# Prompt attention: coefficients transposed whole, masked by VectorE and spread by one 128x512 product

## The reference, cut to what matters

```python
p_c = masked_softmax(jnp.einsum('bqghd,bngd->bghqn', qg, kc) * scale, mask_c)   # 32 compressed keys
o_c = jnp.einsum('bghqn,bngd->bqghd', p_c.astype(vc.dtype), vc)
...
p_s = masked_softmax(jnp.einsum('bqghd,bgqkd->bghqk', qg, kg) * scale, mask_s)  # selected blocks
o_s = jnp.einsum('bghqk,bgqkd->bqghd', p_s.astype(vg.dtype), vg)
...
p_w = masked_softmax(jnp.einsum('bqghd,blgd->bghql', qg, kw) * scale, mask_w)   # last 512 keys
o_w = jnp.einsum('bghql,blgd->bqghd', p_w.astype(vw.dtype), vw)
g = gates.reshape(b, qb, 3, NSA_KV_HEADS, NSA_HG, 1)
o = g[:, :, 0] * o_c + g[:, :, 1] * o_s + g[:, :, 2] * o_w
```

## Time and profile before

| | us |
|---|---|
| runs before | 2155.36, 2158.88, 2159.72 |
| median | 2158.88 |
| the profiled execution | 2153.33 |
| its span, first to last instruction | 2151.6 |
| prompt attention, from its first product to its last scaling | 430.7 to 731.7 |

### The profile page before, as it was taken

One profiled execution on the slowest core, in us unless ns is written; L12 is line 12 of the kernel. 1 busy time (PEld: TensorE's weight loads), 2 busy tenths in 40 slices (PEclk: granted clock), 3 DMA queues, 4 the chain that ended last, 5 costly groups with the idle time before them and its releaser, 6 DMA issues. The chain is left out here.

```text
span 2151.6 us, 25397 instructions
## 1 busy us (share of the span) xinstructions
PE 1876.8 (87%) x10730; PEld 1266.2 (59%) x10730; DVE 693.7 (32%) x1200; ACT 524.9 (24%) x1001; POOL 286.9 (13%) x209
## 2 busy tenths in 40 slices
PE   4499949699889799979997959997999999978795
PEld 4245537366666566656665547774668855534694
DVE  1321110256555234434443231114301124432524
ACT  1400110155444321123343200015311112320004
POOL 1011000011100000024453420000000000010410
PEclk9699979889999899999998979998999999988898
DMA  9101083100000101200001454333110010004312
GB/s 345 72 0 68 1 204 84 42 1 2 1 1 1 44 20 40 98 4 1 1 1 30 124 175 149 110 121 143 40 39 20 20 40 1 1 30 137 120 40 81
DMA packets 116901, 131.83 MB, mean 61 GB/s; under 512 B 15926, under 2 KB 93912, under 8 KB 116148
## 3 DMA queue, kind: packets, MB, share of 16 engines
q1 hardware_dynamic: 95572, 104.94, 15.3%
q10 hardware_dynamic: 20864, 25.17, 3.4%
q0 software_dynamic: 352, 0.10, 0.1%
HBM read 104.83 MB, written 27.43 MB: 61 GB/s over the span
## 5 line engine op out<-in xcount | busy, mean ns | idle before, releaser
L154 PE MATMUL banks<-h_T,w_xbc 128*128 128x352 f32 x576 | 170.9, 460 | 0.0
L154 PE MATMUL banks<-w_attn,h_T 128*128 128x512 f32 (+5 forms) x432 | 160.1, 533 | 0.0
L154 PEld LDWEIGHTS banks<-h_T,w_xbc 128*128 128x128 f32 x576 | 109.5, 190 | 60.9 <-issue 0.6
L154 PE MATMUL banks<-w_r,h_T 128*128 128x512 f32 (+1 forms) x288 | 129.0, 602 | 0.0
L154 PE MATMUL banks<-w_z_b,h_T 128*128 128x512 f32 (+1 forms) x288 | 126.2, 597 | 0.0
L154 PE MATMUL banks<-w_qkv,h_T 128*128 128x256 f32 (+1 forms) x576 | 125.6, 380 | 0.5 <-ACT h_T L2045 0.5
L154 PEld LDWEIGHTS banks<-w_attn,h_T 128*128 128x128 f32 (+1 forms) x432 | 78.5, 183 | 80.3 <-issue 63.5
L154 PEld LDWEIGHTS banks<-w_qkv,h_T 128*128 128x128 f32 (+1 forms) x576 | 103.9, 181 | 22.4 <-issue 2.6
L154 PE MATMUL banks<-h_T,w_qkv 128*128 128x352 f32 x384 | 114.5, 460 | 0.0
L1143 DVE TENSOR_REDUCE neg_max_att<-banks 128x1 f32<-128x640 f32 (+7 forms) x128 | 89.2, 702 | 73.7 <-PE banks L154 73.4
L154 PE MATMUL banks<-conv_T,out_even_w 128*128 128x352 f32 x288 | 92.0, 470 | 14.2 <-DMA out_even_w<-in_w_out_even_dram 12.9
(11 more groups left out here) (427 smaller groups left out, 2977.4 us busy)
## 6 DMA issues: line engine op xcount, KB each, us to landing
out_even_w_mod<-in_w_mod_dram ACTq DMA_DIRECT2D x8, 2048.0 KB, 9.5
h_T<-x_T_save SPq DMA_DIRECT2D x2, 4224.0 KB, 16.8
w_qkv<-in_w_in_odd_dram SPq DMA_DIRECT2D x8, 1024.0 KB, 5.4
w_xbc<-in_w_in_even_dram SPq DMA_DIRECT2D x6, 1024.0 KB, 5.3
x_T_save<-x_T SPq DMA_DIRECT2D x1, 4224.0 KB, 23.6
x_T_save<-h_T SPq DMA_DIRECT2D x1, 4224.0 KB, 19.2
xin<-in_x_prompt_dram SPq DMA_DIRECT2D x2, 2048.0 KB, 16.0
h_T<-in_w_mod_dram SPq DMA_DIRECT2D x2, 2048.0 KB
```

The costliest lines, as they stand in the source:

```text
L154: return nc.tensor.matmul(out, lhsT, rhs, start=start, stop=stop, skip_group_check=True)
```

## The change

`turn_coef` becomes one ordinary transpose of a 128x128 tile: `coef_att` has 128 columns for a block and branch, of which DVE fills the first 8, and POOL sets all to zero once. DVE then multiplies the transposed tile (in PSUM) by a mask into `coef_wide`, 128x512: column block hh keeps the two heads hh and hh+4 (`widen`). A new `spread_coef` is one product with a 0/1 matrix (`half`), contraction over 128 partitions, 512 columns. Mask and matrix lie in a new tile `spread`, 128x132, which SP loads at the start of the stage; PE and DVE wait for it there.

A closing now has two places: the transpose (`turns`) in the unit where the eight products were, the product (`fins`) one unit later. Both stand ahead of `values(n - 1)`. A closing takes two numbers in the counter of groups: the transpose's goes to DVE, the product's to ACT.

```diff
+F_COLS["half"], F_COLS["pick"] = (F_WIDTH + SH, F_WIDTH + SH + P), (F_WIDTH + SH + P, F_WIDTH + SH + P + HG)
...
+    put(f, F_COLS, "half", (p < H)[:, None] & (p[:, None] // HG == p[None, :] // HD))
+    put(f, F_COLS, "pick", (p < H)[:, None] & (p[:, None] % HG == np.arange(HG)[None, :]))
...
-        fins[at["att", i, 0, 0]].append((i, 0))
-        fins[at["att", i, 1, 0]].append((i, 1))
-        fins[at["cmp", i + 1, 0, 0] if i + 1 < NTP else len(units) - 1].append((i, 2))
+        for kind, n in enumerate((at["att", i, 0, 0], at["att", i, 1, 0], at["cmp", i + 1, 0, 0] if i + 1 < NTP else len(units) - 1)):
+            turns[n].append((i, kind))
+            fins[min(n + 1, len(units) - 1)].append((i, kind))
...
+        for eng, table, some in ((0, turning, turns[n]), (1, closing, fins[n])):
+            for f in some:
+                table[f] = len(engine_of)
+                engine_of.append(eng)
...
+        den, coef = sb("den_att", [P, 2, 3, H]), sb("coef_att", [P, 2, 3, P])
+        spread, wide = sb("spread", [P, P + HG]), sb("coef_wide", [P, 2, HG, P])
...
+                sp.dma_start(spread[:, :], e.k_f32[:, F_COLS["half"][0]:F_COLS["pick"][1]]).then_inc(spread_in, 16)
...
                 def turn_coef(i, kind):
 
-                    g = closing[i, kind]
+                    g = turning[i, kind]
                     pe.wait_ge(coef_ready, 3 * i + kind + 1)
                     wait_copied(pe, g - 2)
-                    for hh in range(HG):
-                        for half in range(G):
-                            h = half * HG + hh
-                            c = coef[:, i % 2, kind, h:h + 1].broadcast_to([P, HD])
-                            last = mm(nc, e.ps[half * HD:(half + 1) * HD, 4 + g % 2, hh * P:(hh + 1) * P], c, e.ident, True, True)
-                    last.then_inc(t_done, 1)
+                    nc.tensor.transpose(e.ps[:, 4 + g % 2, 0:P], coef[:, i % 2, kind, :], e.ident).then_inc(t_done, 1)
+
+                def spread_coef(i, kind):
+
+                    g = closing[i, kind]
+                    wait_copied(pe, turning[i, kind])
+                    wait_copied(pe, g - 2)
+                    mm(nc, e.ps[:, 4 + g % 2, :], spread[:, 0:P], wide[:, (3 * i + kind) % 2, :, :].rearrange("p h t -> p (h t)"), True, True).then_inc(t_done, 1)
...
+                pe.wait_ge(spread_in, 16)
                 scores(0)
                 for n in range(len(units)):
                     if n + 1 < len(units):
                         scores(n + 1)
                     turn(n, groups[n])
+                    for f in turns[n]:
+                        turn_coef(*f)
+                    for f in fins[n]:
+                        spread_coef(*f)
                     if n:
                         values(n - 1)
                     if n + 1 == len(units):
                         values(n)
-                    for f in fins[n]:
-                        turn_coef(*f)
...
+                nc.gpsimd.memset(coef[:, :, :, :], 0.0).then_inc(coef_zeroed, 1)
...
+                def widen(i, kind):
+
+                    g = turning[i, kind]
+                    dve.wait_ge(t_done, g + 1)
+                    nc.vector.tensor_tensor(wide[:, (3 * i + kind) % 2, :, :], e.ps[:, 4 + g % 2, 0:P][:, None, :].broadcast_to([P, HG, P]),
+                                            spread[:, P:P + HG][:, :, None].broadcast_to([P, HG, P]), ALU.mult).then_inc(copied_dve, 1)
...
+                dve.wait_ge(coef_zeroed, 1)
+                dve.wait_ge(spread_in, 16)
                 dve.wait_ge(t_done, 1)
...
                     if n in closes:
                         close(n)
+                    for f in turns[n] if n >= 0 else []:
+                        widen(*f)
                     for f in fins[n] if n >= 0 else []:
                         scale(*f)
```

More of the change, by code:

```diff
@@ L81, in shape_constants @@
 def shape_constants():
-    f = np.zeros((P, F_WIDTH + SH), np.float32)
+    f = np.zeros((P, F_COLS["pick"][1]), np.float32)
     p = np.arange(P)
@@ L923, in block_attn_prompt @@
     at = {u: n for n, u in enumerate(units)}
-    fins = {n: [] for n in range(len(units))}
+    turns, fins = {n: [] for n in range(len(units))}, {n: [] for n in range(len(units))}
     for i in range(NTP):
-        fins[at["att", i, 0, 0]].append((i, 0))
-        fins[at["att", i, 1, 0]].append((i, 1))
-        fins[at["cmp", i + 1, 0, 0] if i + 1 < NTP else len(units) - 1].append((i, 2))
+        for kind, n in enumerate((at["att", i, 0, 0], at["att", i, 1, 0], at["cmp", i + 1, 0, 0] if i + 1 < NTP else len(units) - 1)):
+            turns[n].append((i, kind))
+            fins[min(n + 1, len(units) - 1)].append((i, kind))
     closes = {}
@@ L948, in block_attn_prompt @@
     heads_done = [sum(1 if u[0] == "cmp" else 2 for u in units[:n + 1]) for n in range(len(units))]
-    groups, slot, engine_of, order_of, totals, closing = {}, 0, [], [], [0, 0], {}
+    groups, slot, engine_of, order_of, totals, turning, closing = {}, 0, [], [], [0, 0], {}, {}
     engine_of.append(0)
@@ L990, in block_attn_prompt, with _ @@
         with nc.Block() as block:
+            @block.sync
+            def _(sp):
+                sp.dma_start(spread[:, :], e.k_f32[:, F_COLS["half"][0]:F_COLS["pick"][1]]).then_inc(spread_in, 16)
             @block.tensor
@@ L1152, in close @@
                     i, kind = closes[n]
-                    c = coef[:, i % 2, kind, :]
+                    c = coef[:, i % 2, kind, 0:H]
                     dve.wait_ge(p_ready, heads_done[n])
```

8 lines of the change are left out of this document (3 added, 5 removed).

## The result

| | us |
|---|---|
| before, median (4 runs, 2155.36 to 2159.72) | 2157.47 |
| after, median (4 runs, 2179.85 to 2183.31) | 2181.51 |
| ratio after / before, 95% interval | 1.0111 (1.0094 to 1.0129) |
| the profiled execution of after | 2183.31 |
| prompt attention in it, first product to last scaling | 433.55 to 756.62: 323.07 (before 300.32) |

What follows compares the result with a forecast made beforehand. PE, busy 87% of the span, was taken to bound the kernel. Blocks 12.4, start 1.7 and end 1.5 summed to 15.6 us, put on the median of 2158.88: 2174.5 us, range 2163 to 2183.

Steps and rivals of the forecast that it cites:

- rival B: DVE becomes the bound as `widen` delays the next maximum; half of 16.6 us showing gives +24, 2183 us; chance 0.14.
- PE's own work in a closing: On PE, transpose and product take 0.98 us against 0.88 for the eight old products: +0.1 us a closing, no gain.
- The product's wait for copies: Ahead of a unit's values, the product waits for the group two numbers before; 0.5 us a closing in block 3.
- The transpose's wait: No wait given to transposes; in unit 64 one ahead only makes the product wait for the fourth group.
- Blocks: Blocks 0 to 7 of the stage grow by 0, 0.5, 1.8, 1.8, 0.9, 1.6, 2.7 and 3.1 us: 12.4 us.
- Kind 2's old place: Block 7, unit 63: the old products cost nothing there, since PE waited 1.54 us after them for exponentials.
- DVE, ACT and POOL: `widen` takes 0.69 us, 16.6 in all, mostly hidden; ACT's copy is unchanged; POOL's clearing runs beside the load of `spread`.
- The start: PE waits for the DMA of `spread` ahead of the first scores, at 432.9 instead of 431.23: +1.7 us (1.0 to 2.3).
- The end: The last values wait for coefficients, transpose, `widen` and product; `scale` starts at 732.5 instead of 731.01: +1.5 us (1.0 to 2.5).
- A: Rival: waits are hidden, products cost only 0.1 us each; +5.6, 2164.5 us; chance 0.20 together with the overhead rule.
- C: Rival: faster, block 4 to 7 closings fall into waits, copy waits and low clock at 453.5 vanish; -4.4, 2154.5; chance 0.04.
- D: Rival: the change changes nothing but start and end, +3 us, 2162; chance 0.09, shared with any result within 4.3 us.

Runs made afterwards that it cites:

- e5: Changed kernel with transpose and product both behind their units' values, and the wait for `spread` only ahead of first users; 2166.98 us, ratio to before 1.0034.
- e1: Changed kernel with only the product `spread_coef` moved behind its unit's values, the transpose staying ahead; 2172.04 us, ratio to before 1.0061.
- e6: Changed kernel with every transposed group copied by the engine that copied it before the change; one run of 2177.72 us.
- e7: Changed kernel in which DVE does each `widen` twice, first into a spare tile nobody reads; one run of 2183.68 us.
- e4: Changed kernel with PE and DVE waiting for `spread` only ahead of the first product and first `widen`; one run of 2177.85 us.
- e9: Changed kernel, unedited, profiled once more; single run of 2179.87 us.
- e10: Changed kernel, unedited, profiled yet again; single run of 2184.53 us.
- e3: Changed kernel with only the very last unit's transpose and product put behind its values; one run of 2177.12 us.
- e2: Kernel before with a closing's eight products moved ahead of the values in the same unit; 2160.84 us, ratio to before 1.0012.
- e8: Kernel before with four transposes replacing a closing's eight products, DVE writing each coefficient 64 times wide; 2155.21 us, ratio to before 0.9988.

## Why the prediction was right in sign and short by 7 us

Slower was forecast with 0.87, and the time lies in the range; the likeliest value was 2174.5, the measured one is 2181.5. The stage is 22.8 us longer, where 15.6 were forecast; the difference of 24.0 between the medians is larger by what the median before moved with a fourth run, 1.4 us. That the range holds the time is in part luck. The band given to the forecast's own mechanism was +11 to +20, and the measured +24.0 lies beyond it, where the prediction had put rival B with 0.14; B's mechanism is not what happened, but the room left for it is what kept the time inside. Step by step:

**PE's own work in a closing: +0.1 forecast, +0.1 to +0.25 measured.** A record of the product has a median of 0.595 us, and both together last 1.02 to 1.10 at the high clock, so the second starts 0.43 to 0.5 us behind the first, against 0.44 from the earlier trace rows. In e5 a product adds 0.96 us to its unit, not 0.87; the rest is probably the turn from other shapes and back, which I left out. No gain for PE, as forecast. The Trainium skill (TensorEngine Tiling (Array Packing), Instruction Overhead) counts about 60 cycles for each matmul. By that the 312 records fewer should save 312 x 60 / 2.4 GHz = 7.8 us, as an estimate from that page; PE is busy 9.1 us longer instead, some 3 us of it at the low clock of the end, and in e5 the three records of a closing take 1.0 to 1.1 us where sixteen took 0.86. Read as a price for each record, the rule does not hold for these products.

**The product's wait for copies: right in kind.** Unit 24 waits 0.76 us, where I took 0.5: I read the wait from a unit with eight blocks to turn (unit 28) and used it for one with six, which turn 0.22 us sooner. In unit 29, of eight, the wait is 0.53 (521.77 less 520.22, less 1.02 for the transposes): as read.

**The transpose's wait: the step that failed.** The prediction says that the product "stands ahead of the unit's values, so PE waits there", and it gives the transpose no wait except in unit 64, where it counted only as what pushes the product's wait to the fourth group. But the transpose has the same `wait_copied(pe, g - 2)` in the same place. It waits 0.55 us in unit 19, 0.66 in unit 23, 0.63 in unit 28, 0.33 in unit 32, 0.64 in unit 55 and 0.73 in unit 64; the group of `const_f,coef_att` in after shows 5.2 us ahead of transposes in all, of which 0.8 is the end. Where a product stands right behind such a transpose (units 19, 28, 55, 64) it waits no more, so a block does not have three waits, one for each product, but four: in block 3 the transposes of units 28 and 32 and the products of units 29 and 33. e5 against e1 gives the price: without the transposes' waits blocks 2 and 3 are 1.5 and 1.3 us shorter, nearly all of the 3.0 us that the forecast lacks there. In the old place a transpose costs 0.05 to 0.17 us.

**Blocks.** Forecast 0, 0.5, 1.8, 1.8, 0.9, 1.6, 2.7, 3.1, in all 12.4. Measured -0.2, -0.4, +3.4, +3.2, +1.3, +2.7, +2.7, +3.8, in all 16.5. Blocks 2 and 3 carry 3.0 of the 4.1 us missing, and these have no slack to hide the transposes' waits. Block 1 is better than forecast: the low clock from 453.5 us never comes (unit 9 1.69 us instead of 3.98), which pays for unit 10 (+1.5) and part of unit 11 (+0.9). Unit 65 was forecast at 8.8 and is 8.87, unit 64 at 7.9 and is 8.1 to 8.3.

**Kind 2's old place: no gain, as forecast.** Unit 63 is unchanged, only PE's wait behind it grew from 1.54 to 2.31 us. The same holds for unit 45 (5.06 and 5.05 us). Unit 54 fell from 5.64 to 5.31, but unit 53 ahead of it grew by as much, and with the copies split as before (e6) both are what they were.

**DVE, ACT and POOL: right.** `widen` has a median of 0.682 us, forecast 0.69, and e7 shows a second one mostly hidden. POOL's clearing (0.74 us) lies inside the load.

**The start: +1.7 forecast, +1.4 measured.** e4 gives it back.

**The end: +1.5 forecast, +4.8 measured (3.3 and 4.8 in e9 and e10).** The order of events was right, the term was sized with durations at 2.4 GHz. With the clock up it is +1.1 to +1.6 (e6, e1, e3). The idle time that I had written down myself, for coefficients, transpose and `widen`, lets the clock fall, and product and values then run at 1.2 GHz. The kernel before put that idle time behind the last values, where nothing long followed.

**Rivals.** A (waits hidden) is refuted by the 9.5 us of waits for copies ahead of the new steps. B is refuted by e7, so far as the second `widen` speaks for the first. C's point was a copy done within 0.1 us of the last transpose; it is 0.5 to 0.8 late. But one part of C came true: the low clock at 453.5 us is absent in all eleven profiles of other kernels here. With one profile of the kernel before, it is not shown that the edit is the reason. D is refuted by the table. So the sum went wrong in two terms: the blocks, by 4.1 us (the transposes' waits, at most 4.4 us, and the turn to the product, with slack in blocks 4 to 7 taking some of it back), and the end, by 3.3, for the clock.

## What to carry to other kernels

Where a change splits one step into two, charge both with the wait that stood ahead of the one; an instruction of 0.1 us in the wrong place waited up to 0.7 us here, nearly as long as one of 0.9 us (0.8). An instruction that waits for a copy of what has just been turned belongs behind the next products that need nothing, not ahead of them. And at the end of a stage put the engine's last long work into the wait for the other engine: in e3 that hid the wait and kept the clock.

## What was not expected of the hardware

- **The clock after idle time is not the same in each run.** After the 2.31 us of idle ahead of unit 64, the first 2.5 us of it ran at a granted clock of 1.00 in after, e1, e9 and e10, 0.80 in e3, 0.68 in e4, 0.65 in e6 and 0.50 in e7, for units of 8.1 to 9.6 us. After and e3 have the same work up to there, and so has e4 from block 1 on, so it is not the order of work that decides. Where PE had been idle for less (1.54 us in before and e2, 1.83 in e8, 2.15 in e5) no loss was seen in that unit. But e5 had one in unit 53, where none of the idle times before it was over 0.56 us. What decides is open. Two windows, of e6 and of e7:

```profile
701.26:703.76 2.50, 2.50 (x10) 0.65 0.00 0
```

```profile
701.52:704.02 2.50, 2.50 (x8) 0.50 0.04 7
```

- **A transpose of 128x128 float32 is one record of 0.11 us, where the products here are two records each.** Four of them (0.49 us) do the work of eight products of 64 output columns (0.86 us) and of a product of 512 columns (0.96 us). Duplication through DVE's broadcast, 0.52 us more on an engine with time to spare, was cheaper than any form of it on PE.
